# Two projection stages joined: branch and merge gates as one plan of units, each of seven products

## The chip, the cores and the metric

The kernel runs on one core of a Trainium2 chip. The metric is the device time of one execution in microseconds. Shown are the median of three executions and one profiled execution, from which all durations are read.

## The reference, cut to what matters

All of it is in float32, with 2048 latent tokens, width 1024 and two mixers (branches a and b) of 4 heads of 128. The part around the change is the end of the first block:

```
u = layer_norm(x) * (1 + scale) + shift
a_gate, b_gate, merge = columns of (u @ w_in)          # 512, 512 and 2 * 1024 columns
def rms_norm_gated(o, gain, gate):
    return o * rsqrt(mean(o * o) + eps) * gain * silu(gate)
y_a = rms_norm_gated(o_a, a_norm_g, a_gate) @ w_a_out    # o_a, o_b: the mixers' outputs, per head
y_b = rms_norm_gated(o_b, b_norm_g, b_gate) @ w_b_out
gates = sigmoid(merge.reshape(tokens, 2, 1024))
sub = (gates[0] * y_a + gates[1] * y_b) @ w_out
```

Each mixer runs in two directions, and `o_a`, `o_b` are the sums of the two outputs. After this comes a residual, and a second block that the change leaves alone.

## The kernel before, in words

The program is a chain of phases. Each is a block in which every engine has its own hand-written instruction stream, in the order of the code, with waits on counting semaphores; a new block starts on all engines when the old one has ended. PE is TensorE, DVE is VectorE, ACT is ScalarE, POOL is GpSimd, and SP issues most DMAs. A name as `T.at(v, "m4")` is the semaphore value that stands once product m4 of unit v is done. `bank` is PSUM: 8 banks of 128x512 float32.

`uT` holds u, with 8 blocks of 128 rows by 256 context and 2048 latent tokens. Its context columns hold weights by the time of these phases. `phase_scans` loads the first weights there (`wg_saved`) at its end. `yT` receives the normed, turned outputs: 8 heads by 2048 tokens.

**Branch gates** (`phase_branch_gates`). For each of 8 heads f and 4 blocks b of 512 tokens, PE does 8 matmuls (L1614, one for each block of 128 rows of u) and ACT a Silu (L1660). Meanwhile 32 groups of the mixers' outputs are normed. A group goes through these steps: SP loads its two directions (`outputs`, tiles `o` and `other`), DVE adds them (L1668), ACT squares (L1634), DVE reduces, scales and inverts (L1672 to L1677), ACT takes the root (L1637), DVE multiplies (L1681), PE turns it with 4 transposes (L1622) into one of 4 banks, and ACT copies it with the gain into `yT` (L1649). PE turns two groups after each block from the second to the seventeenth. DVE then multiplies `yT` by the Silu (L1689), and SP saves the second half of the tokens to DRAM (`y_d`).

**Merge gates** (`phase_merge_gates`). Here a unit is 256 output columns by 1024 tokens (a half), so 2 by 2 blocks on each side of a product. They are made with seven products of 4 matmuls (Strassen's scheme in Winograd's form, `PRODUCTS`) where eight would be the plain way. POOL makes four sums of the weights (L1769 to L1774) into `S`, which has two buffers; DVE makes four sums of the tokens once for each half (L1833 to L1842), in spare space of `yT`; PE does the products (L1787) and takes a new bank only when that of eight products ago is read; ACT keeps a copy of m1 (L1811); DVE combines the products (L1853 to L1869); ACT applies the Sigmoid (L1820) and stores to `sig_d`. There are 16 units: 8 on the first half of the tokens, 8 on the second.

After it, `phase_merge` uses `yT` and `sig_d`.

## Time and profile before

| | |
|---|---|
| median of 3 executions | 4029.23 us (4026.57 to 4033.26) |
| profiled execution, its own time | 4030.66 us |
| its span | 4028.9 us |
| TensorE busy | 3772.0 us, 94% of the span |
| branch gates | from 1501.7 us on |
| merge gates | from 1747.2 us to 2137.9 us |

The span is that of the instructions in the profile; 1.8 us of the execution's time lie around it. Each float32 matmul stands in the trace as two records (256 matmuls of the branch gates are 512 records), a transpose as one. A matmul's recorded duration overlaps the next one's: the pitch from start to start is what a product costs.

### The profile page before, as it was taken

Reading aid. Unit: us, or ns where it says so; the run is one execution under the profiler, and the core shown is the slowest. Engines: PE = TensorE matmul, PEld = TensorE weight load, DVE = VectorE, ACT = ScalarE, POOL = GpSimd, SP = SyncE. Lnnn points to the kernel's source line nnn. Section 1 sums busy time; section 2 is a strip of 40 time slices with the busy share of each in tenths; the row PEclk is TensorE's granted clock in tenths of the full one; section 3 lists DMA queues with packets and bytes.
Section 4 is the critical chain, followed back from the end, with each engine's and each line's share of the span. In section 5 each row is a group of like instructions: output and inputs, shape, how many; then the busy total and the mean of one; then the engine's idle time right before and its main releaser. Section 6 shows DMA issues by size and latency. Waiting matters only on the chain. (4 is left out here: it accounts for less than half of the span.)

```text
span 4028.9 us, 48826 instructions
## 1 busy us (share of the span) xinstructions
PE 3772.0 (94%) x18971; PEld 1980.1 (49%) x18971; DVE 2214.4 (55%) x3725; ACT 1204.6 (30%) x2355; POOL 727.5 (18%) x660
## 2 busy tenths in 40 slices
PE   6999899999799989999999989899998999999898
PEld 3444354444577764444444434343554355565543
DVE  7688426653466655222225877622456466565578
ACT  3333123454355547301110001111222244444300
POOL 0000000000566650022113332223110000000032
PEclk8999999999899999999999999999998999999999
DMA  5122673567645544222324633321101100000133
GB/s 189 47 50 49 112 150 112 112 123 127 172 158 175 180 140 141 82 73 84 125 84 146 230 105 120 118 96 68 48 32 37 35 1 8 8 1 6 58 125 110
DMA packets 590152, 386.33 MB, mean 96 GB/s; under 512 B 412019, under 2 KB 525783, under 8 KB 586979
## 3 DMA queue, kind: packets, MB, share of 16 engines
q1 hardware_dynamic: 573059, 315.57, 28.4%
q0 software_dynamic: 10336, 42.47, 2.9%
q10 hardware_dynamic: 6528, 25.17, 1.6%
q8 instruction: 152, 2.49, 0.3%
q14 instruction: 77, 0.63, 0.1%
HBM read 252.59 MB, written 130.55 MB: 95 GB/s over the span
## 5 line engine op out<-in xcount | busy, mean ns | idle before, releaser
L632 PE MATMUL bank<-uT,front_W 128*128 128x512 f32 (+1 forms) x1216 | 489.3, 564 | 4.4 <-ACT front_b_ L839 4.4
L564 PE MATMUL bank<-uT,front_W 128*128 128x512 f32 (+1 forms) x896 | 363.5, 564 | 0.0
L632 PEld LDWEIGHTS bank<-uT,front_W 128*128 128x128 f32 x1216 | 232.7, 192 | 252.6 <-issue 246.0
L564 PEld LDWEIGHTS bank<-uT,front_W 128*128 128x128 f32 x896 | 170.0, 191 | 183.1 <-issue 179.8
L3245 PE MATMUL bank<-kT,attn_qT 96*128 96x512 f32 (+3 forms) x640 | 248.6, 540 | 7.6 <-ACT kT L3305 6.8
L1614 PE MATMUL bank<-uT 128*128 128x512 f32 x512 | 224.3, 596 | 4.3 <-PEq L1183 4.3
L3245 PEld LDWEIGHTS bank<-kT,attn_qT 96*128 96x128 f32 x640 | 114.1, 190 | 131.2 <-issue 74.7
L1313 POOL TENSOR_TENSOR scan_U<-scan_U,gla_w 128x512 f32<-128x512 f32 x144 | 146.9, 1041 | 168.8 <-DVE scan_U L1501 168.8
L3365 DVE TENSOR_SCALAR_CACHE_REDUCE attn_sc_big<-bank 128x512 f32<-128x512 f32 (+1 forms) x208 | 125.9, 627 | 72.9 <-PE bank L3245 71.0
L1614 PEld LDWEIGHTS bank<-uT 128*128 128x128 f32 x512 | 96.5, 191 | 119.8 <-issue 119.8
L1303 POOL TENSOR_TENSOR scan_SP<-scan_S,eGl 128x512 f32<-128x512 f32 x144 | 146.9, 1041 | 19.9 <-DVE scan_S L1520 13.6
L3388 DVE COPY attn_pT<-bank 128x512 f32<-128x512 f32 (+1 forms) x184 | 110.3, 635 | 70.8 <-PE bank L3260 70.8
L3314 ACT ACTIVATE attn_sc_big<-attn_sc_big,attn_top 128x1920 f32<-128x1920 f32 (+3 forms) x64 | 104.3, 1629 | 111.2 <-DVE attn_top L3377 111.2
L1009 DVE RECIPROCAL front_q<-front_q 128x2048 f32<-128x2048 f32 (+1 forms) x8 | 110.0, 13752 | 47.5 <-ACT front_q L786 47.5
L3273 PE MATMUL bank<-attn_pT,uT 128*64 128x256 f32 (+1 forms) x1152 | 129.9, 372 | 5.2 <-DVE attn_pT L3388 5.2
L3479 POOL TENSOR_TENSOR out_S<-uT,out_b 128x512 f32<-128x512 f32 x8 | 13.1, 1639 | 671.0 <-DVE uT L3559 671.0
L1520 DVE TENSOR_TENSOR scan_S<-scan_SP,bank 128x512 f32<-128x512 f32 x144 | 92.5, 685 | 63.4 <-PE bank L1395 63.4
L1001 DVE SCALAR_TENSOR_TENSOR front_work<-front_work,front_taps 128x2308 f32<-128x2308 f32 (+1 forms) x48 | 121.6, 2533 | 1.7
L479 POOL TENSOR_TENSOR front_work<-front_neg_beta,ctri 128x256 f32<-128x256 f32 x18 | 13.1, 750 | 594.3 <-DVE front_neg_beta L1065 510.6
L1787 PE MATMUL bank<-yT,merge_S 128*128 128x512 f32 x256 | 116.8, 599 | 2.3 <-POOL merge_S L1774 2.3
L3260 PE MATMUL bank<-ident,attn_sc_big 128*128 128x128 f32 x800 | 103.3, 281 | 15.9 <-DVE attn_pT L3388 12.6
L1820 ACT ACTIVATE merge_r<-merge_r 128x1024 f32<-128x1024 f32 x32 | 33.7, 1052 | 266.6 <-DVE merge_r L1867 264.2
(547 smaller groups left out, 7070.8 us busy)
## 6 DMA issues: line engine op xcount, KB each, us to landing
scan_gq<-gla_asks_keys_values SPq DMA_DIRECT2D x36, 768.0 KB, 7.7
scan_dq<-delta_qkv SPq DMA_DIRECT2D x32, 768.0 KB, 6.2
merge_gates<-merge_r ACTq DMA_DIRECT2D x16, 1024.0 KB
uT<-merge_gates SPq DMA_DIRECT2D x16, 1024.0 KB, 8.8
gla_asks_keys_values<-front_a SPq DMA_DIRECT2D x14, 1152.0 KB, 11.0
front_W<-in_w_in SPq DMA_DIRECT2D x28, 512.0 KB, 10.7
delta_qkv<-front_b_ SPq DMA_DIRECT2D x8, 1152.0 KB, 9.9
gla_asks_keys_values<-front_b_ SPq DMA_DIRECT2D x8, 1152.0 KB, 17.8
```

The costliest lines, as they stand in the source:

```text
L564: m = pe.matmul(bank[:, conv_bank(f, b), 0:n], W[:, f % 2, k, :], uT[:, k, t0:t0 + n], start=(k == 0), stop=(k == KT - 1))
L632: mm = pe.matmul(bank[:, b, 0:n], W[:, s, k, :], uT[:, k, t0:t0 + n], start=(k == 0), stop=(k == KT - 1))
L1001: dve.scalar_tensor_tensor(out=acc[:, lo:WIDE], in0=raw[:, f % 2, lo + t:t + WIDE], scalar=tap[:, t:t + 1], in1=acc[:, lo:WIDE], op0=ALU.m ...
L1009: dve.reciprocal(inv[:, r], inv[:, r]).then_inc(DY("inv"), 1)
L1303: nc.gpsimd.tensor_tensor(SP[d][:], S[d][:], bcast(gl, 2, P), ALU.mult).then_inc(GS(f"SP{d}"), 1)
L1313: nc.gpsimd.tensor_tensor(U[d][:], U[d][:], bcast(w, 2, P), ALU.mult).then_inc(GU(f"U{d}"), 1)
L1614: mm = pe.matmul(bank[:, b, :], W[f % 2][:, k, :], uT[:, k, CTX + b * BANK:CTX + (b + 1) * BANK], start=(k == 0), stop=(k == KT - 1))
L1787: mm = pe.matmul(bank[:, spot(q, name), :], left[:, k, :], right(k), start=(k == 0), stop=(k == H - 1))
L3245: pe.matmul(bank[:, SC0 + ring[name] % NS, 0:hi - lo], qT[:, e, i * P:(i + 1) * P], kT[0:QK, e, lo:hi], start=True, stop=True).then_inc(TS ...
L3273: m = pe.matmul(bank[e * DV:(e + 1) * DV, ob, r0:2 * P], vall[:, c, h * DV:(h + 1) * DV], pT[:, n % NPT, e, r0:2 * P], start=(c == 0), sto ...
L3365: m = dve.tensor_scalar(t[:, g * BANK:g * BANK + w], bk[:, 0:w], SCALE, None, ALU.mult, ALU.max, accum_out=mx[:, s, u, plain:plain + 1])
L3388: dve.tensor_copy(*turned_spot(a, p, c)).then_inc(DT(name), 1)
```

## The change

`phase_branch_gates` and `phase_merge_gates` become one block, `phase_gates`, driven by a list `PLAN` of 24 units of the same shape: 8 merge units of the first half of the tokens, then 8 branch units (a pair of heads by a half), then 8 merge units of the second half. So the branch gates' projections are made in seven products too. The norming and turning of the 32 groups is spread over the first products: step k stands at product 3k/2 (`slot_of`), that is two steps in each three products, with PE's transposes of group k - 3 behind that product. The sum of the two directions moves from DVE to POOL. The transposes have 2 banks and the products 6. `S` has one buffer, and POOL waits for products m5 and m3 of the unit before. The token sums lie in tiles `T1`, `T2`, `T4` of their own and are rebuilt at the three places where the plan turns to the other half (`TURNS`: units 10, 14, 16).

```diff
+    BRANCH = [(0, 0), (1, 0), (1, 1), (0, 1), (2, 1), (3, 1), (3, 0), (2, 0)]
+    merge = lambda g: [("merge", br, j, g) for br in range(2) for j in range(COLS)]
+    PLAN = merge(0) + [("branch", p // (HEADS // 2), p, g) for p, g in BRANCH] + merge(1)
+    UNITS, NBU = len(PLAN), len(BRANCH)
...
+    SLOT = [v % 2 for v in range(NM)] + [0, 1, 1, 0, 1, 0, 0, 1] + [v % 2 for v in range(NM)]
+    SUMS = ["new"] * NM + ["new", "new", "", "again", "new", "new", "", "again"] + ["new"] * NM
+    TURNS = [v for v in range(1, UNITS) if half_of(v) != half_of(v - 1)]
...
+    slot_of = lambda k: 3 * k // 2
+    steps_at = lambda x: [k for k in range(ALL + 3) if slot_of(k) == x]
...
-        W = [uT[:, :, s * P:(s + 1) * P] for s in range(2)]
+        W = [uT[:, :, 0:2 * P], WM]
+        S = sb("S", [P, 3, H, P])
+        T1, T2, T4 = (sb(n, [P, H, BANK]) for n in ("T1", "T2", "T4"))
...
-        sq = sb("sq", [P, 2, GC, P])
...
-        silu = sb("silu", [P, 2, SEQ])
+        r = sb("r", [P, 2, 2, PAIR])
...
+        spot = lambda v, name: (7 * v + PRODUCTS.index(name)) % 6
...
-        @block.gpsimd
-        def _(pool):
-            nc.clear_and_free_semaphores(chip.ended)
...
+                    sp.wait_ge(DI.sem, DI.at(i - 2, "ss"))
...
+            for x in range(7 * UNITS):
+                v, i = divmod(x, 7)
+                for k in steps_at(x):
+                    if 2 <= k + 1 < ALL:
+                        outputs(k + 1)
+                if i == 0:
+                    for n, (w, after) in enumerate(LOADS):
+                        if after is not None and after == v - 1:
+                            weights(n)
...
+            nc.clear_and_free_semaphores(chip.ended)
...
+                    weights_here(pool, v)
+                    if v:
+                        pool.wait_ge(T.sem, T.at(v - 1, "m5"))
+                    pool.tensor_tensor(S[:, 0], w21, w22, ALU.add).then_inc(GW("s1"), 1)
+                    pool.wait_ge(GW.sem, GW.at(n, "s1"))
+                    pool.tensor_tensor(S[:, 1], S[:, 0], w11, ALU.subtract).then_inc(GW("s2"), 1)
+                    pool.tensor_tensor(w21, w11, w21, ALU.subtract).then_inc(GW("s3"), 1)
+                    if v:
+                        pool.wait_ge(T.sem, T.at(v - 1, "m3"))
+                    pool.wait_ge(GW.sem, GW.at(n, "s2"))
+                    pool.tensor_tensor(S[:, 2], w12, S[:, 1], ALU.subtract).then_inc(GW("s4"), 1)
...
+            weights(0)
+            for x in range(7 * UNITS):
+                for i in steps_at(x):
                     if i < ALL:
-                        outputs(i)
-                if B % NB == NB - 1 and B // NB + 2 < NF:
-                    weights(B // NB + 2)
...
-            for f in range(NF):
-                pe.wait_ge(w_loaded[f % 2], f // 2 * 16 + 16)
-                for b in range(NB):
...
-                    for i in turned(f * NB + b):
...
+            def turned(i):
...
+                    tr = pe.transpose(bank[:, 6 + i % 2, c * P:(c + 1) * P], o[:, i % 4, c, :], chip.ident[:])
+                tr.then_inc(TT("turned"), 1)
...
+                x = 7 * v + PRODUCTS.index(name)
+                if x >= 6:
+                    reader, value = taken[PRODUCTS[(x - 6) % 7]]
+                    pe.wait_ge(reader.sem, reader.at((x - 6) // 7, value))
+                for k in range(H):
+                    mm = pe.matmul(bank[:, spot(v, name), :], left[:, k, :], right[:, k, :], start=(k == 0), stop=(k == H - 1))
+                mm.then_inc(T(name), 1)
+                for k in steps_at(x):
+                    if k >= 3:
+                        turned(k - 3)
...
+                weights_here(pe, v)
+                product(v, "m1", w11, u(g, LO, 0))
+                product(v, "m2", w12, u(g, HI, 0))
+                if SUMS[v] == "new":
+                    pe.wait_ge(GW.sem, GW.at(n, "s3"))
+                elif SUMS[v]:
+                    pe.wait_ge(GA.sem, GA.at(n, "s1"))
...
+                if fresh:
+                    pe.wait_ge(DT.sem, DT.at(i, "t2"))
+                product(v, "m6", S[:, 1], T2)
...
+                if SUMS[v] == "new":
+                    pe.wait_ge(GW.sem, GW.at(n, "s4"))
...
+                product(v, "m3", S[:, 2], u(g, HI, 1))
+                if fresh:
+                    pe.wait_ge(DT.sem, DT.at(i, "t4"))
+                product(v, "m4", w22, T4)
...
-                    act.wait_ge(DS.sem, DS.at(i, "sum"))
-                    if i >= 2:
-                        act.wait_ge(DI.sem, DI.at(i - 2, "ss"))
-                    act.activation(sq[:, i % 2], o[:, i % 4], ACT.Square).then_inc(AQ("sq"), 1)
+                    act.wait_ge(GS.sem, GS.at(i, "sum"))
+                    act.activation(other[:, i % 2], o[:, i % 4], ACT.Square).then_inc(AQ("sq"), 1)
...
-            for f in range(NF):
-                for b in range(NB):
-                    B = f * NB + b
-                    for i in (2 * B, 2 * B + 1):
-                        norm(i)
-                    for i in turned(B):
-                        turn(i)
-                    act.wait_ge(T.sem, T.at(f, f"proj{b}"))
-                    if f >= 2:
...
+            for x in range(7 * UNITS):
+                v, i = divmod(x, 7)
+                for k in steps_at(x):
+                    if k >= 3:
+                        turn(k - 3)
+                    norm(k)
+                if i == 0:
+                    keep(v)
+                    if v:
+                        gate(v - 1, 1)
+                if i == 6:
+                    gate(v, 0)
...
-                if i < ALL:
-                    dve.wait_ge(o_loaded[i % 4], i // 4 * 32 + 32)
-                    dve.tensor_tensor(o[:, i % 4], o[:, i % 4], other[:, i % 2], ALU.add).then_inc(DS("sum"), 1)
...
+            def gated(v):
+                _, br, p, g = PLAN[v]
+                dve.wait_ge(AT.sem, AT.at(NG * (1 + br) - 1, "turned"))
+                dve.wait_ge(AS.sem, AS.at(v, "gate1"))
+                y = yT[:, 2 * p:2 * p + 2, g * PAIR:(g + 1) * PAIR]
+                dve.tensor_tensor(y, y, r[:, v % 2], ALU.mult).then_inc(DY("y"), 1)
...
+            for x in range(7 * UNITS):
+                v, i = divmod(x, 7)
+                for k in steps_at(x):
+                    norm(k)
+                if x == 1:
+                    last_sum(0)
+                if x == 3:
+                    difference(1)
+                combine(v, PRODUCTS[i])
+                if i == 2 and v and is_branch(v - 1):
+                    gated(v - 1)
+                if v + 1 in TURNS:
+                    g, n = half_of(v + 1), TURNS.index(v + 1) + 1
+                    if PRODUCTS[i] == "m7":
+                        second_sum(g)
+                    if PRODUCTS[i] == "m3":
+                        first_sum(g, n)
+                    if PRODUCTS[i] == "m4":
+                        last_sum(g)
```

The next rows are TensorE's, at the start of the branch gates (before) and of the joined block (after). L1614 and L1622 are a block's matmuls and the transposes, as above.

```order
L1606 UNCONDITIONAL_BRANCH
L1614 MATMUL bank<-uT 128x512 x16
L1622 MATMUL bank<-ident,gates_o 128x128 x8
L1614 MATMUL bank<-uT 128x512 x8
L1622 MATMUL bank<-ident,gates_o 128x128 x8
L1614 MATMUL bank<-uT 128x512 x8
```

```order
L1710 UNCONDITIONAL_BRANCH
L1726 MATMUL bank<-uT 128x512 x8
L1726 MATMUL bank<-gates_T,gates_S 128x512 x4
L1726 MATMUL bank<-uT 128x512 x4
L1726 MATMUL bank<-gates_T,gates_S 128x512 x4
L1717 MATMUL bank<-ident,gates_o 128x128 x4
L1726 MATMUL bank<-uT,gates_S 128x512 x4
L1726 MATMUL bank<-gates_T,uT 128x512 x4
L1717 MATMUL bank<-ident,gates_o 128x128 x4
L1726 MATMUL bank<-uT,WM 128x512 x4
L1717 MATMUL bank<-ident,gates_o 128x128 x4
L1726 MATMUL bank<-uT,WM 128x512 x4
```

The transposes (now L1717) came in eights behind every block of 8 matmuls; now they come in fours, behind two of each three products of 4 matmuls (L1726). Ahead of the first of them stand five products.

The next rows are GpSimd's, from the same place. The ISA row clears semaphores; before, the second branch is the start of the merge gates, some 250 us later.

```order
L1570 UNCONDITIONAL_BRANCH
L1572 ISA
L1544 UNCONDITIONAL_BRANCH
L1761 UNCONDITIONAL_BRANCH
L1769 TENSOR_TENSOR merge_S<-WM 128x512
L1771 TENSOR_TENSOR merge_S<-merge_S,WM 128x512
L1772 TENSOR_TENSOR WM<-WM 128x4x128
L1774 TENSOR_TENSOR merge_S<-WM,merge_S 128x512
L1769 TENSOR_TENSOR merge_S<-merge_W 128x512
L1771 TENSOR_TENSOR merge_S<-merge_S,merge_W 128x512
L1772 TENSOR_TENSOR merge_W<-merge_W 128x4x128
L1774 TENSOR_TENSOR merge_S<-merge_W,merge_S 128x512
```

```order
L1672 UNCONDITIONAL_BRANCH
L1674 ISA
L1685 TENSOR_TENSOR gates_S<-uT 128x512
L1687 TENSOR_TENSOR gates_S<-gates_S,uT 128x512
L1688 TENSOR_TENSOR uT<-uT 128x4x128
L1692 TENSOR_TENSOR gates_S<-uT,gates_S 128x512
L1706 TENSOR_TENSOR gates_o<-gates_o,gates_other 128x512 x5
L1685 TENSOR_TENSOR gates_S<-WM 128x512
L1687 TENSOR_TENSOR gates_S<-gates_S,WM 128x512
L1688 TENSOR_TENSOR WM<-WM 128x4x128
L1692 TENSOR_TENSOR gates_S<-WM,gates_S 128x512
L1706 TENSOR_TENSOR gates_o<-gates_o,gates_other 128x512 x5
```

The first weight sums (L1685 to L1692) now stand directly behind the clear, and the sums of the mixers' outputs (L1706) stand between the weight sums of one unit and those of the next.

The last rows are ScalarE's: before, in the branch gates; after, around the end of the second merge unit. L1782 copies a turned group, L1767 squares, L1770 is the root, L1788 keeps m1, L1792 is the gate's function and L1797 stores.

```order
L1649 ACTIVATE yT<-bank,gates_gain 128x4x128 x2
L1660 ACT_TABLE_LOAD
L1660 ACTIVATE gates_silu<-bank 128x512
L1634 ACTIVATE gates_sq<-gates_o 128x512
L1637 ACT_TABLE_LOAD
L1637 ACTIVATE gates_ss<-gates_ss 128x4
L1634 ACTIVATE gates_sq<-gates_o 128x512
L1637 ACTIVATE gates_ss<-gates_ss 128x4
```

```order
L1792 ACT_TABLE_LOAD
L1792 ACTIVATE gates_r<-gates_r 128x1024
L1788 ACTIVATE gates_kept<-bank 128x512
L1792 ACTIVATE gates_r<-gates_r 128x1024
L1797 DMA merge_gates<-gates_r 128x2x1024
L1782 ACTIVATE yT<-bank,gates_gain 128x4x128
L1767 ACTIVATE gates_other<-gates_o 128x512
L1770 ACT_TABLE_LOAD
L1770 ACTIVATE gates_ss<-gates_ss 128x4
L1782 ACTIVATE yT<-bank,gates_gain 128x4x128
L1767 ACTIVATE gates_other<-gates_o 128x512
L1770 ACTIVATE gates_ss<-gates_ss 128x4
```

The Silu of a block between steps has gone; the two Sigmoids of a unit and the copy of m1 stand there in its place.

## Rows read from the trace of the kernel before

**Rows 1.** The page: the span, and TensorE (busy us, share, instructions).

```profile
span 4028.9 us, 48826 instructions
PE 3772.0 (94%) x18971; PEld 1980.1 (49%) x18971; DVE 2214.4 (55%) x3725; ACT 1204.6 (30%) x2355; POOL 727.5 (18%) x660
```

**Rows 2.** Timeline of TensorE, branch gates: start, us, what, count.

```profile
1501.72 15.67 PE L1614 MATMUL bank<-uT 128*128 128x512 f32 x32 [4.26 <-PEq L1183]
1517.22 1.04 PE L1622 MATMUL bank<-ident,gates_o 128*128 128x128 f32 x8
1518.10 7.03 PE L1614 MATMUL bank<-uT 128*128 128x512 f32 x16
```

**Rows 3.** Waits, 1480 to 2260 us: total, times, longest, in us.

```profile
PE bank L1622 <- DVE gates_o L1681: 5.4, 8, 1.5
```

**Rows 4.** Timeline of TensorE, merge gates: its first unit and its last product.

```profile
1747.20 8.80 PE L1787 MATMUL bank<-uT,WM 128*128 128x512 f32 x16 [2.15 <-PEq L1544]
1758.31 5.32 PE L1787 MATMUL bank<-yT,merge_S 128*128 128x512 f32 x8 [2.31 <-POOL merge_S L1774]
1763.47 3.60 PE L1787 MATMUL bank<-uT,WM 128*128 128x512 f32 x8
1777.20 5.31 PE L1787 MATMUL bank<-uT,merge_W 128*128 128x512 f32 x12
...
2134.27 3.60 PE L1787 MATMUL bank<-merge_T,merge_W 128*128 128x512 f32 x8
```

**Rows 5.** Windows: length, busy us of PE, PEld, DVE, ACT, POOL; PEclk; DMA.

```profile
1500.00:1505.00 5.00, 3.28 (x5) 1.51 (x6) 0.00 (x0) 0.00 (x0) 0.39 (x1) 0.72 0.42 133
1760.00:1765.00 5.00, 5.00 (x11) 2.19 (x10) 1.70 (x3) 0.00 (x0) 4.92 (x4) 0.84 0.00 0
1501.70:1745.10 243.40, 237.86 (x640) 110.68 (x640) 90.21 (x191) 115.18 (x162) 0.00 (x0) 0.99 0.32 102
```

**Rows 6.** GpSimd and VectorE: timeline rows, and the semaphore clear.

```profile
1751.68 3.31 POOL L1772 TENSOR_TENSOR WM<-WM 128x512 f32<-128x512 f32 x1
1878.67 2.28 DVE L1836 TENSOR_TENSOR uT<-uT 128x2048 f32<-128x2048 f32 x1
1878.88 3.20 POOL L1769 TENSOR_TENSOR merge_S<-WM 128x512 f32<-128x512 f32 x1 [18.85 <-DMA WM<-in_w_in]
1882.16 1.26 POOL L1771 TENSOR_TENSOR merge_S<-merge_S,WM 128x512 f32<-128x512 f32 x1
L1572 POOLq EVENT_SEMAPHORE_RANGE_CLEAR  x1: 439/439/439, 1501.8 to 1501.8; - x1
```

**Rows 7.** ScalarE in the branch gates: groups (busy, mean ns), then timeline.

```profile
L1649 ACT ACTIVATE yT<-bank,gates_gain 128x512 f32<-128x512 f32 x32 | 27.7, 909 | 13.0 <-PE bank L1622 12.8
L1637 ACT ACT_TABLE_LOAD x17 | 21.8, 1283 | 0.3
L1634 ACT ACTIVATE gates_sq<-gates_o 128x512 f32<-128x512 f32 x32 | 20.1, 627 | 22.8 <-DVE gates_o L1668 22.4
1509.59 1.28 ACT L1637 ACT_TABLE_LOAD   x1
1510.89 0.20 ACT L1637 ACTIVATE gates_ss<-gates_ss 128x4 f32<-128x4 f32 x1
```

**Rows 8.** VectorE, groups of 1495 to 2160 us: busy, mean ns, idle before.

```profile
L1672 DVE TENSOR_REDUCE gates_ss<-gates_sq 128x4 f32<-128x512 f32 x32 | 21.7, 679 | 0.4 <-ACT gates_sq L1634 0.4
L1681 DVE TENSOR_TENSOR gates_o<-gates_o,gates_ss 128x512 f32<-128x512 f32 x32 | 21.2, 663 | 5.6 <-ACT gates_ss L1637 5.6
L1677 DVE RECIPROCAL gates_ss<-gates_ss 128x4 f32<-128x4 f32 x32 | 5.7, 178 | 1.1
L1855 DVE TENSOR_TENSOR merge_r<-bank,merge_kept 128x512 f32<-128x512 f32 x16 | 11.1, 692 | 42.0 <-PE bank L1787 42.0
```

**Rows 9.** DMA issues: count, KB each, median us to landing.

```profile
gates_other<-mixer_outputs SPq DMA_DIRECT2D x32, 256.0 KB, 3.2
WM<-in_w_in SPq DMA_DIRECT2D x7, 1024.0 KB, 5.3
```

More of the change, by code:

```diff
@@ L1543, in phase_branch_gates @@
     ALL = 2 * NG
+    COLS = DM // (2 * P)
+    BRANCH = [(0, 0), (1, 0), (1, 1), (0, 1), (2, 1), (3, 1), (3, 0), (2, 0)]
+    merge = lambda g: [("merge", br, j, g) for br in range(2) for j in range(COLS)]
+    PLAN = merge(0) + [("branch", p // (HEADS // 2), p, g) for p, g in BRANCH] + merge(1)
+    UNITS, NBU = len(PLAN), len(BRANCH)
+    NM = 2 * COLS
+    half_of = lambda v: PLAN[v][3]
+    is_branch = lambda v: PLAN[v][0] == "branch"
+    nth = lambda v: [w for w in range(UNITS) if is_branch(w) == is_branch(v)].index(v)
+    SLOT = [v % 2 for v in range(NM)] + [0, 1, 1, 0, 1, 0, 0, 1] + [v % 2 for v in range(NM)]
+    SUMS = ["new"] * NM + ["new", "new", "", "again", "new", "new", "", "again"] + ["new"] * NM
+    TURNS = [v for v in range(1, UNITS) if half_of(v) != half_of(v - 1)]
+    LOADS = [(v, max([w for w in range(v) if SLOT[w] == SLOT[v]], default=None)) for v in range(1, UNITS) if SUMS[v] == "new"]
+    LOADS.sort(key=lambda load: -1 if load[1] is None else load[1])
+    arrivals = {}
+    for n, (v, after) in enumerate(LOADS):
+        arrivals[v] = 16 * (2 + sum(SLOT[w] == SLOT[v] for w, a in LOADS[:n]))
+    slot_of = lambda k: 3 * k // 2
+    steps_at = lambda x: [k for k in range(ALL + 3) if slot_of(k) == x]
     with ExitStack() as st:
@@ L1574, in _, with weights @@
         @block.sync
         def _(sp):
-            def weights(f):
-                if f >= 2:
-                    sp.wait_ge(T.sem, T.at(f - 2, f"proj{NB - 1}"))
-                base = C_AGATE if f < HEADS else C_BGATE - HD
-                sp.dma_start(W[f % 2], w_in[:, base + f * P:base + (f + 1) * P].rearrange("(k p) n -> p k n", p=P)
-                             ).then_inc(w_loaded[f % 2], 16)
+            def weights(n):
+                v, after = LOADS[n]
+                if after is not None:
+                    sp.wait_ge(T.sem, T.at(after, "m4"))
+                kind, br, p, g = PLAN[v]
+                if kind == "branch":
+                    c = (C_AGATE if br == 0 else C_BGATE - HD) + 2 * p * P
+                else:
+                    c = C_MERGE + br * DM + p * 2 * P
+                sp.dma_start(W[SLOT[v]], w_in[:, c:c + 2 * P].rearrange("(k p) n -> p k n", p=P)
+                             ).then_inc(w_loaded[SLOT[v]], 16)
@@ new lines, in _, with weights @@
+            sp.wait_ge(T.sem, T.at(UNITS - 2, "m4"))
+            for br, w in enumerate((w_a_out, w_b_out)):
+                sp.dma_start(uT[:, br * HEADS:(br + 1) * HEADS, 0:2 * P], w[:, 0:2 * P].rearrange("(k p) n -> p k n", p=P)
+                             ).then_inc(wy_loaded, 16)
+            sp.wait_ge(wy_loaded, 32)
+            sp.wait_ge(y_loaded, 16 * 2 * HEADS)
+        @block.gpsimd
+        def _(pool):
+            nc.clear_and_free_semaphores(chip.ended)
+            def weights(v):
+                if not SUMS[v]:
+                    return
+                w11, w12, w21, w22 = quarters(v)
+                n = SUMS[:v].count(SUMS[v])
+                if SUMS[v] == "new":
[10 more added lines that the diff above has]
+                    pool.tensor_tensor(S[:, 2], w12, S[:, 1], ALU.subtract).then_inc(GW("s4"), 1)
+                else:
+                    pool.wait_ge(T.sem, T.at(v - 1, "m5"))
+                    pool.tensor_tensor(S[:, 1], w22, w21, ALU.subtract).then_inc(GA("s2"), 1)
+                    pool.wait_ge(GA.sem, GA.at(n, "s2"))
+                    pool.tensor_tensor(S[:, 0], S[:, 1], w11, ALU.add).then_inc(GA("s1"), 1)
+                    pool.wait_ge(T.sem, T.at(v - 1, "m3"))
+                    pool.tensor_tensor(S[:, 2], w12, S[:, 1], ALU.subtract).then_inc(GA("s4"), 1)
+            weights(0)
+            for x in range(7 * UNITS):
+                for i in steps_at(x):
+                    if i < ALL:
+                        pool.wait_ge(o_loaded[i % 4], i // 4 * 32 + 32)
+                        pool.tensor_tensor(o[:, i % 4], o[:, i % 4], other[:, i % 2], ALU.add).then_inc(GS("sum"), 1)
+                if x % 7 == 6 and x // 7 + 1 < UNITS:
+                    weights(x // 7 + 1)
@@ new lines, in product @@
+            def product(v, name, left, right):
+                x = 7 * v + PRODUCTS.index(name)
[8 more added lines that the diff above has]
+                        turned(k - 3)
@@ L1671, in norm @@
                     dve.wait_ge(AQ.sem, AQ.at(n, "sq"))
[L1672 removed]
+                    dve.tensor_reduce(ss[:, n, 0, :], other[:, n % 2], AX.X, ALU.add).then_inc(DI("ss"), 1)
                     dve.wait_ge(DI.sem, DI.at(n, "ss"))
```

335 lines of the change are left out of this document (120 added, 215 removed).

## The prediction

> **What bounds the kernel now.** I read the page first: TensorE is busy 3772.0 of 4028.9 us, no other engine above 55% [rows 1]. Then the timeline of TensorE over the two stages: it runs from 1501.72 us to the end of the last product, 2134.27 + 3.43 = 2137.70 us, with hardly a gap [rows 2, 4]. In the branch gates it is busy 237.86 of 243.40 us [rows 5]. So this stretch of 636.0 us costs what TensorE's instructions cost, plus a few named waits, and a change here is worth what it does to TensorE's instructions and to those waits. The other engines matter only where they are late.
>
> **The pitch of a product.** From the start of m1 of the second merge unit (1777.20) to the start of the last m4 (2134.27) are 357.07 us and 104 products [rows 4]: 3.433 us a product, 0.858 us a matmul, 24.03 us a unit. The branch gates' matmuls have the same size (128x128 by 512), and I give them the same price.
>
> **Where the 636.0 us go before.** Branch gates, 243.4 us: 256 matmuls x 0.858 = 219.7. The first 16 of them took 1517.22 - 1501.72 = 15.50 where 13.73 is the price, 1.8 too much; the granted clock of that time is 0.72 of full in the first window, so TensorE was for a part of it at 1.2 GHz, after it had stood still for 4.26 us [rows 2, 5]. Transposes: 8 in 1518.10 - 1517.22 = 0.88 us, 0.44 a group, 14.1 for 32 groups [rows 2]. What is left, 7.8 us, is waiting: 5.4 us are booked as waits of the transposes for VectorE's scaled group [rows 3]; the other 2.4 I take for refilling behind them. Merge gates: 2.15 us at the block's boundary. The first unit took 1777.20 - 1747.20 = 30.00 us, 5.97 over its price: m1 and m2 8.80 for 6.87, a wait of 2.31 for GpSimd's weight sums, and m6 5.16 for 3.43 [rows 4], the granted clock being still at 0.84 behind that wait [rows 5]. Then 15 units x 24.03 = 360.5. Sum: 243.4 + 2.15 + 30.0 + 360.5 = 636.05, as the timeline has it.
>
> **What the change removes on TensorE.** The same projections in 24 units of 28 matmuls are 672 for 256 + 448 = 704: 32 matmuls, 27.5 us. The 32 groups of transposes stay, 14.1 us. They now stand alone in fours where they came in eights; if all of the 2.4 us above is really the price of breaking the stream, they cost 16.5. I take 14.1, since in the rows with no wait the eight cost only 0.88.
>
> **The start, which stays once.** One of two starts goes, with its 2.15 us boundary. The remaining one looks like the merge gates' start. m1 and m2 cost 15.50 - 6.87 = 8.6 us (to 1510.35) for 6.87, so 1.8 over. GpSimd clears semaphores until 1502.2 [rows 6], then makes three sums before m6 may start. VectorE makes three token sums of 2.28 us at the same time. The rows show what such a meeting does: a GpSimd sum that takes 1.26 us alone took 3.20 when it began 0.2 us behind a VectorE sum of 2.28, and 3.31 in the merge gates' start [rows 6]. In turns, GpSimd ends at about 1505.3, 1508.8 and 1512.3. So m6 waits 2.0 us, and then has m6's 1.7 us of low clock again. Start cost: 1.8 + 2.0 + 1.7 = 5.5 us. Bounds: 1.8 if GpSimd is in time, 8.1 if it costs what the merge gates' start did with its boundary.
>
> **What is laid beside TensorE, and whether it stays there.** During the steps a unit costs TensorE 24.03 + 4.67 groups x 0.44 = 26.1 us. *VectorE*: a step is 0.68 + two small ones of about 0.18 + 0.66 = 1.7 us, and a unit has 4.67 of them and seven combining operations of 0.69 [rows 8]: 12.8 us. *ScalarE*: 4.67 x (0.91 + 0.63 + 0.20) = 8.1, the copy of m1 and two Sigmoids about 2.7 together (0.6 and twice 1.05, by size), and three table loads of 1.28 [rows 7], 3.9: 14.7 us. *GpSimd*: four weight sums of 1.27 and 4.67 output sums of at most the same: 11 us. None is a bound by its load; what counts is order. I cost at nothing, with its cover: the weights' loads (5.3 us to landing [rows 9], one unit of 24 us to land in); the weight sums with one buffer (allowed from the end of m5, wanted by m6 four products or 13.7 us later, 3.8 us of work); the token sums at the three turns (2.28 us each, wanted five products later); the products' six banks (a reader has five products, 17 us, where it had seven); the branch units' multiplications and saves; the loads for the next stage, issued one unit before the end. Without its cover each would stop TensorE for its own length.
>
> **The tight places.** (1) Group 0 is turned behind the fifth product. By my count its sum comes behind the four weight sums (1514.7), its square at 1515.3, VectorE then makes a token sum and two combinations, and the scaled group is there at 1523. TensorE is there at 1512.4 + 5.2 + 6.9 = 1524.5: 1.5 us of slack. (2) In units 1 and 4 the output sum of the seventh product's step stands on GpSimd ahead of the next unit's weight sums. Counted from the end of m5: a load may start at 3.9 (behind m3 and a turned group) and lands near 7.8 (two issues, then 3.2 us [rows 9]), the output sum ends at 9, three weight sums at 12.8 to 13; m6 wants them at 15.1. Two us of slack. (3) SP issues a unit's weights behind a step's loads, which wait for the turned group: at most 4 us late, of some 18 spare. For (1) to (3) together I set 1.0 us of waiting.
>
> Whether a scaling multiply of 0.66 us (a tile and a broadcast column, both in SBUF) also blocks GpSimd is in no row. The Trainium skill, "SBUF — State Buffer", its part on engine ports, says that any VectorE instruction with two SBUF inputs and a GpSimd instruction that reads SBUF exclude each other for the whole instruction; by it each multiply that meets a sum adds up to 0.66 us, 3.1 us over a unit, and place (2) would lose most of its slack. A second rule speaks against ScalarE: "ScalarE: Activation LUTs", What ACT_TABLE_LOAD costs, gives 2.66 us for a switch of tables, a drain of 1.38 included. Here the load begun at 1509.59 lasts 1.28, and the root starts at 1510.89, right behind it [rows 7]: this trace does not show that drain. With it ScalarE's unit would be 18.8 us, still below 26.1, but its burst at a unit's edge would be longer than the distance to the next step.
>
> **Sum.** After: 576.7 + 14.1 + 5.5 + 1.0 = 597.3. Before: 636.05. Gain 38.7 us: 27.5 from matmuls, 6.8 from the transposes' waits, 4.4 from the starts (1.8 + 2.15 + 5.97 - 5.5). From the profiled execution's 4030.66 us that gives 3992.0. That execution stands 1.4 us above the median of the three, so by the median 3990.5. I say 3991.
>
> **The rivals.**
> *A, the forecast*: TensorE stays the bound. With the bounds above (start 1.8 to 8.1, transposes 14.1 to 16.5, waits 0 to 3) the gain is 32 to 43 us: 3986 to 3997. Chance 0.75.
> *B, the cover is thin*: a GpSimd sum or a scaled group is late in several of the seven mixed units, and each wait also lowers the clock. Priced by the merge gates' start, 2.31 + 1.73 = 4.0 us a time; at three places 12 us, 4003; at all seven 28 us, 4019. For it: slacks of 1.5 to 2 us, against an estimate with as much error. Against it: no load above 60% of the unit, and every queue can catch up. Chance 0.2, most of it near 4000.
> *C, slower*: the steps' loop itself is too long. `o` has four buffers, so group i + 4 is loaded only when group i is turned, and four steps are six products, 20.6 + 1.8 = 22.4 us. Bare, the loop is 0.8 issue + 3.2 landing + 1.3 + 0.6 + 1.1 + 1.5 + 0.7 = 9.2 us. Each engine holds other work ahead of it (GpSimd up to 5 us of weight sums, ScalarE 4, VectorE 3). If queueing made it 30 us, TensorE would wait 7.6 us each four steps, 61 us in 32 steps: 4052. It turns slower than before from a loop of 27.3 us on (39 us of waiting). Chance 0.03.
> *D, nothing gained beyond the matmuls*: the starts and waits stay what they were and only 27.5 us go: 4002, inside B's span. *E*: the first unit hardly waits, and the gain is 43 us or more: 0.02.
>
> **Range and chances.** 3986 to 4001 leaves out C, the upper part of B and a little of A. A measurement of this kernel tells 0.2%, 8 us, from no change. Faster by more: A, E and nearly all of B, 0.96; within: 0.02; slower: C's larger part, 0.02.
>
> **What would show it right or wrong.** The product pitch in all 24 units at 3.43 us; TensorE's stretch from m1 of unit 0 to the last m4 near 597 us and 672 matmuls; m6 of unit 0 waiting about 2 us for a GpSimd sum, with the granted clock near 0.8 around it; waits of the transposes for the scaled group near nothing; a unit in the mixed part at 26.1 us. Wrong would be: units 1 to 6 longer than 27 us, with waits on `gates_S` or `gates_o` (B), or the wait of every step's loads on SP handed through to TensorE (C); a pitch above 3.43; or a next stage that begins with a longer gap.

## The result and the profile after

The changed kernel took 3985.55 us (median of 4 runs, 3984.27 to 3988.39), the kernel before, on the same chip, 4029.55 us (4 runs, 4026.57 to 4033.26). The ratio is 0.9891, 95% interval 0.9874 to 0.9908: 44.0 us less. The prediction was 3991, its range 3986 to 4001: the time lies just below the range. The profiled execution took 3984.89 us, its span is 3983.1.

The page of the changed kernel, the lines that answer to [rows 1]:

```profile
span 3983.1 us, 48748 instructions
PE 3738.3 (94%) x18907; PEld 1965.4 (49%) x18907; DVE 2257.9 (57%) x3731; ACT 1188.4 (30%) x2336; POOL 789.7 (20%) x714
```

There are 64 TensorE records fewer, two for each of the 32 matmuls that are gone, and 54 more on GpSimd, mostly the 32 output sums. TensorE's busy time fell by 33.7 us, the span by 45.8: the rest of the gain is standing time.

The timeline of TensorE in the changed kernel: the start of the joint stage, its last product, and the first instructions of the next two stages.

```profile
1501.79 8.77 PE L1726 MATMUL bank<-uT 128*128 128x512 f32 x16 [4.50 <-PEq L1183]
1511.56 3.70 PE L1726 MATMUL bank<-gates_T,gates_S 128*128 128x512 f32 x8 [1.00 <-POOL uT L1688]
1515.09 3.60 PE L1726 MATMUL bank<-uT 128*128 128x512 f32 x8
1518.53 3.60 PE L1726 MATMUL bank<-gates_T,gates_S 128*128 128x512 f32 x8
1521.96 0.60 PE L1717 MATMUL bank<-ident,gates_o 128*128 128x128 f32 x4
1522.40 3.60 PE L1726 MATMUL bank<-uT,gates_S 128*128 128x512 f32 x8
...
2092.21 3.60 PE L1726 MATMUL bank<-gates_T,WM 128*128 128x512 f32 x8
2102.16 4.23 PE L2028 MATMUL bank<-yT,uT 128*128 128x512 f32 x5 [6.36 <-PEq L1568]
2311.45 2.04 PE L2251 MATMUL bank<-yT 128*128 128x512 f32 x2 [10.75 <-PEq L1914]
```

Read the starts: 1515.09, 1518.53, 1521.96 are 3.43 us apart, the pitch of a product as before [rows 4], and the four transposes between 1521.96 and 1522.40 cost 0.44. The stretch from the first m1 to the end of the last m4 is 2092.21 + 3.43 - 1501.79 = 593.85 us, where [rows 2, 4] give 635.98.

The same next stages in the kernel before, from the timeline of TensorE:

```profile
2144.26 4.33 PE L1995 MATMUL bank<-yT,uT 128*128 128x512 f32 x6 [6.40 <-PEq L1713]
2355.81 2.05 PE L2218 MATMUL bank<-yT 128*128 128x512 f32 x2 [10.74 <-PEq L1881]
```

From these rows the span's 45.8 us divide by place. From the first m1 to the next stage's first matmul: 642.54 against 600.37 us, 42.2 gained. That next stage to the following one: 211.55 against 209.29, 2.3 gained. Everything behind it: 4028.9 - 2355.81 = 1673.09 against 3983.1 - 2311.45 = 1671.65, 1.4 gained. The change's own stretch holds 42.2; the other 3.7 are in stages whose work it doesn't touch (0.1 us was lost ahead of the stretch).

The waits of the changed kernel, 1495 to 2110 us (total, times, longest):

```profile
PEld bank L1717 <- DVE gates_o L1830: 0.2, 1, 0.2
POOL gates_o L1706 <- DMA gates_other<-mixer_outputs: 85.6, 23, 8.6
ACT gates_other L1767 <- POOL gates_o L1706: 33.0, 11, 17.5
```

Where [rows 3] had 5.4 us of transposes waiting for the scaled group, 0.2 is left. GpSimd stands 85.6 us for the mixers' outputs, up to 8.6 at a time. ScalarE, which squares a group next, waits for these sums in turn (33.0 us), but the groups are still ready when TensorE comes, so none of this waiting reaches TensorE. Who waits for a load turned out to be the point of the experiments below.

### The profile page after: what moved, and what is told of

The parts are those of the page before. It is cut to its first block and busy times, and to the rows that moved or that the text cites. A ratio compares the mean times of both kernels' runs of the same rounds, so it can differ in the third digit from the quotient of the medians.

```text
span 3983.1 us, 48748 instructions
## 1 busy us (share of the span) xinstructions
PE 3738.3 (94%) x18907; PEld 1965.4 (49%) x18907; DVE 2257.9 (57%) x3731; ACT 1188.4 (30%) x2336; POOL 789.7 (20%) x714
## 3 DMA queue, kind: packets, MB, share of 16 engines
q8 instruction: 151, 2.47, 0.3%
## 5 line engine op out<-in xcount | busy, mean ns | idle before, releaser
L1726 PE MATMUL bank<-gates_T,gates_S 128*128 128x512 f32 x384 | 172.7, 592 | 1.0 <-POOL uT L1688 1.0
L1726 PE MATMUL bank<-uT 128*128 128x512 f32 x288 | 129.6, 599 | 4.5 <-PEq L1183 4.5
L1792 ACT ACTIVATE gates_r<-gates_r 128x1024 f32<-128x1024 f32 x48 | 50.6, 1054 | 270.0 <-DVE gates_r L1879 267.5
L1726 PE MATMUL bank<-uT,WM 128*128 128x512 f32 x288 | 128.0, 592 | 0.0
```

Source lines behind the costliest of these rows:

```text
L1726: mm = pe.matmul(bank[:, spot(v, name), :], left[:, k, :], right[:, k, :], start=(k == 0), stop=(k == H - 1))
```

## The experiments

In all of them "the stretch" is the time from the first m1 (in the kernel before, the first matmul of the branch gates) to the end of the last m4, by the timeline of TensorE. One execution of the changed kernel has 593.85 us of it, the other 593.94 (below), so differences of 0.5 us in it can be read, where the medians of whole runs scatter by several us.

**Both kernels once more.** No edit. The kernel before, one run:

> The kernel before, unchanged, for a second profile. The change gained 42.1 us between the first product of the gates and the last, and 3.7 us more behind it (2.2 of them in the stage that follows, 200.2 against 197.9 us from its first to its last product). Theory (chance): the stages behind the gates differ from one execution to the next by 1 to 3 us, in waits for DMA, so this profile shows the stage behind the gates anywhere from 197.5 to 200.5 us. Rival (the change speeds up what follows): again 200.2 within 0.4 us.

It took 4029.3 us. Its stretch begins with the same record and ends 2132.92 + 3.43 = 2136.35, 635.3 us long. The start of its merge gates, in the timeline of TensorE, differs from [rows 4]:

```profile
1745.77 7.10 PE L1787 MATMUL bank<-uT,WM 128*128 128x512 f32 x16 [2.15 <-PEq L1544]
1756.88 5.40 PE L1787 MATMUL bank<-yT,merge_S 128*128 128x512 f32 x8 [4.01 <-POOL merge_S L1774]
1762.12 3.60 PE L1787 MATMUL bank<-uT,WM 128*128 128x512 f32 x8
2142.92 4.65 PE L1995 MATMUL bank<-yT,uT 128*128 128x512 f32 x6 [6.40 <-PEq L1713]
2354.36 2.05 PE L2218 MATMUL bank<-yT 128*128 128x512 f32 x2 [10.73 <-PEq L1881]
```

The same boundary of 2.15 us did not slow m1 and m2 here (7.10 us; in [rows 4] 8.80). They ended 1.7 us earlier, and m6 then waited 1.7 us longer (4.01 for 2.31) for the same GpSimd sum: from m1 to m6 are 11.11 us in both. So the low clock of m1 and m2 was no cost of its own: the sums set the start. What cost was the sum's lateness and m6's own low clock.

The changed kernel, four runs:

> The changed kernel, unchanged, for a second profile and a narrower interval. Both theories: 3985.5 us within 1.5, the gates' stretch 593.9 us within 0.5. Theory (chance): the stage behind the gates takes anywhere from 197.5 to 200.5 us. Rival (the change speeds up what follows): 197.9 again within 0.4, and the time behind the last product of the gates is 3.5 us shorter than in both profiles of before.

3985.36 us (3983.43 to 3989.32) against 4026.3 (4024.04 to 4028.14), ratio 0.9897 [0.988, 0.9913]; here the gain is 40.9 us. Rows of the timeline of TensorE:

```profile
1502.26 8.74 PE L1726 MATMUL bank<-uT 128*128 128x512 f32 x16 [4.42 <-PEq L1183]
1512.12 3.70 PE L1726 MATMUL bank<-gates_T,gates_S 128*128 128x512 f32 x8 [1.12 <-POOL uT L1688]
2092.77 3.60 PE L1726 MATMUL bank<-gates_T,WM 128*128 128x512 f32 x8
2102.72 4.59 PE L2028 MATMUL bank<-yT,uT 128*128 128x512 f32 x6 [6.35 <-PEq L1568]
2314.39 2.05 PE L2251 MATMUL bank<-yT 128*128 128x512 f32 x2 [10.76 <-PEq L1914]
```

The gates' start repeats, and the next stage does not: 2314.39 - 2102.72 = 211.67 us in this execution of the same kernel, 209.29 in the first, 211.55 and 211.44 in the two of the kernel before. The kernel before with its output sums on GpSimd (below) has 209.07 us there. What came out 2.3 us better behind the gates in the first pair is scatter from execution to execution, not the change; the last section shows where in that stage it arises. Between this pair the gain up to the next stage's start is 641.88 - 600.46 = 41.4.

**Is it the matmuls?** The 32 matmuls are put back: each of the eight branch units makes its m1 (4 matmuls) twice.

```
-                for k in range(H):
-                    mm = pe.matmul(bank[:, spot(v, name), :], left[:, k, :], ...)
+                for again in range(2 if name == "m1" and is_branch(v) else 1):
+                    for k in range(H):
+                        mm = pe.matmul(bank[:, spot(v, name), :], left[:, k, :], ...)
```

> In the eight branch units product m1 is made twice, the second time over the first, so the joined stage has the 704 matmuls that the two stages had. Theory (the 32 matmuls are worth their pitch of 0.858 us and nothing else): 27.5 us slower than the changed kernel, 4013, and still 14.5 us faster than before; the gates' stretch 621.4 us. Rival (the eight-product form was not priced at the seven-product pitch, or part of the 27.5 hides in waits): under 25 or over 30 us.

4013.72 us (4013.1 to 4017.0, 6 runs) against 4026.46 (15 runs), ratio 0.9967 [0.9955, 0.998]. The stretch runs from 1503.45 to 2121.43 + 3.43, 621.41 us: 27.5 more than without. So 27.5 us of the gain are the matmuls; the 12.7 us that this kernel is still faster (by the stretch 14.6, against the first profile of the kernel before) are the rest, waits and starts.

**The wait of m6 in the first unit.** In the changed kernel m6 waits for the third of the sums that GpSimd makes. Here it waits for the fourth in unit 0.

```
-                    pe.wait_ge(GW.sem, GW.at(n, "s3"))
+                    pe.wait_ge(GW.sem, GW.at(n, "s3" if v else "s4"))
```

> In unit 0 alone TensorE waits for the fourth weight sum before m6, not for the third, as the merge gates did before. The fourth ends 1.2 us later, so the wait before m6 grows from 1.0 to 2.2 us. Theory (a longer wait brings the low clock with it, as in the kernel before: 2.31 us of waiting, then 1.7 us lost in m6): 2.9 us slower, 3988.5, m6 of unit 0 at 5.2 us and not 3.5. Rival (the low clock came from what TensorE did before the block began, not from this wait): 1.2 us slower, 3986.8, m6 at 3.5 us.

3987.16 us (3985.95 to 3988.7), ratio 0.9903 [0.9888, 0.9918]. TensorE's timeline:

```profile
1512.61 3.70 PE L1726 MATMUL bank<-gates_T,gates_S 128*128 128x512 f32 x8 [2.19 <-POOL gates_S L1692]
1516.14 3.60 PE L1726 MATMUL bank<-uT 128*128 128x512 f32 x8
```

A standstill of 2.19 us, and m6 behind it takes 1516.14 - 1512.61 = 3.53, the full rate. The stretch grew by 1.2 us, the wait alone. The prediction's step "a wait of two us brings 1.7 us of low clock" does not hold here.

**Longer waits at the same place.** Two kernels in which m6 of unit 0 also waits for GpSimd's first output sum (the first expectation) or second (the second):

```
+                if v == 0:
+                    pe.wait_ge(GS.sem, GS.at(0, "sum"))      # second kernel: GS.at(1, "sum")
```

> In unit 0, m6 waits besides for GpSimd's first sum of the mixers' outputs, so TensorE stands still for some 3.4 us and not 1.0 after its first 16 records. Waits of 1.0 and 2.2 us there left the clock at full and m6 at 3.53 us; a wait of 4.0 us in the second profile of before cost m6 5.24 us. Theory (the clock falls by the length of the standstill, and the bound lies between 2.2 and 4.0): m6 either 3.5 or 5.2 us, the gates' stretch 2.4 or 4.1 us longer than 593.5. Rival (at this place the clock does not fall, since what counts is something else than the wait): m6 3.5 here and in the next kernel too.

> The same with GpSimd's second sum: a standstill of some 4.6 us. Theory (a standstill of 4 us or more brings the low clock): m6 about 5.2 us and not 3.5, the gates' stretch 3.6 + 1.7 = 5.3 us longer than 593.5. Rival: m6 3.5 us, the stretch 3.6 us longer.

One run each: 3984.93 and 3991.81 us. The timeline of TensorE in the first:

```profile
1511.08 3.67 PE L1726 MATMUL bank<-gates_T,gates_S 128*128 128x512 f32 x8 [3.01 <-issue]
1514.59 3.60 PE L1726 MATMUL bank<-uT 128*128 128x512 f32 x8
```

In the second:

```profile
1513.94 5.37 PE L1726 MATMUL bank<-gates_T,gates_S 128*128 128x512 f32 x8 [4.77 <-issue]
1519.15 3.60 PE L1726 MATMUL bank<-uT 128*128 128x512 f32 x8
```

And the window of the second at the start of m6 (columns as in [rows 5]):

```profile
1514.00:1516.00 2.00, 2.00 (x3) 0.88 (x4) 1.93 (x4) 1.97 (x3) 0.00 (x0) 0.56 0.42 114
```

A standstill of 3.01 us left the clock full (m6 3.51); one of 4.77 us ended with m6 at 5.21 and a granted clock of 0.56 in this window, near the lower of the two levels (1.2 GHz of 2.4). The stretch grew by 2.4 and 5.4 us. In the first that is 2.0 of added wait and 0.5 of m1 and m2, which took 9.24 us in this execution; in the second 3.8 of wait and 1.7 of clock.

**Removing the wait of m6.** VectorE makes its third token sum only behind GpSimd's third weight sum:

```
             second_sum(0)
+            dve.wait_ge(GW.sem, GW.at(0, "s3"))
             first_sum(0, 0)
```

> VectorE makes its third token sum only when GpSimd has made its third weight sum, in unit 0 alone. Theory (the two engines exclude each other, so the third weight sum then takes 1.27 us and not 3.3): it is ready at about 1509.5, m6 starts with no wait at 1510.6, 1.0 us faster: 3984.5; the groups behind are not late. Rival (the sum is slow for another reason, or the token sum comes too late for m5 and moves the wait there): no gain, 3985.5 or slower.

3985.46 us (3983.79 to 3986.67), ratio 0.9898 [0.9883, 0.9913]. GpSimd's timeline in the changed kernel:

```profile
1502.28 2.69 POOL L1685 TENSOR_TENSOR gates_S<-uT 128x512 f32<-128x512 f32 x1 [2.06 <-POOLq L1183]
1505.04 3.19 POOL L1687 TENSOR_TENSOR gates_S<-gates_S,uT 128x512 f32<-128x512 f32 x1
1508.20 3.31 POOL L1688 TENSOR_TENSOR uT<-uT 128x512 f32<-128x512 f32 x1
```

And with the edit, the third sum and TensorE:

```profile
1499.95 8.80 PE L1726 MATMUL bank<-uT 128*128 128x512 f32 x16 [4.41 <-PEq L1183]
1506.45 1.26 POOL L1688 TENSOR_TENSOR uT<-uT 128x512 f32<-128x512 f32 x1
1508.59 3.60 PE L1726 MATMUL bank<-gates_T,gates_S 128*128 128x512 f32 x8
```

The third sum took 1.26 us where it took 3.31, and m6 started behind m2 without a wait. The stretch is 592.98 us, the shortest of all, 0.9 less. The medians of whole runs (3985.46 and 3985.36) cannot tell 1 us, so this is the better version by its trace alone.

**What the move of the output sums to GpSimd is worth, twice.** First in the kernel before: its direction sums go to GpSimd, which was idle there.

```
+            for i in range(ALL):
+                pool.wait_ge(o_loaded[i % 4], i // 4 * 32 + 32)
+                pool.tensor_tensor(o[:, i % 4], o[:, i % 4], other[:, i % 2], ALU.add).then_inc(DS("sum"), 1)
...
             def norm(i):
-                if i < ALL:
-                    dve.wait_ge(o_loaded[i % 4], i // 4 * 32 + 32)
-                    dve.tensor_tensor(o[:, i % 4], o[:, i % 4], other[:, i % 2], ALU.add).then_inc(DS("sum"), 1)
```

> The kernel before with one part of the change alone: the sum of the two directions of the mixers' outputs on GpSimd, idle in that stage, and not on VectorE. Theory (the transposes' waits of before came from the pairs of groups behind one block of 6.9 us, that is from the spacing of the steps): the waits shrink by at most half, 1 to 4 us faster than before. Rival (they came from VectorE's load): all 7.8 us go, 7 us or more faster.

4023.39 us (4019.91 to 4027.77, 10 runs) against 4026.46, ratio 0.9994 [0.9985, 1.0004]: no difference that can be told. The transposes wait less (the waits, 1480 to 2260 us, that answer to [rows 3]):

```profile
PE bank L1625 <- DVE gates_o L1681: 3.8, 4, 1.4
```

From the first matmul to the boundary it needs 241.4 us, the two executions of the kernel before 243.3 and 242.6: 1.2 to 1.9 us less. That is the theory's size, not the rival's 7 us or more.

Then in the changed kernel: the sums go back to VectorE, ahead of the step's other work (removed from GpSimd's loop).

```
             def norm(i):
+                if i < ALL:
+                    dve.wait_ge(o_loaded[i % 4], i // 4 * 32 + 32)
+                    dve.tensor_tensor(o[:, i % 4], o[:, i % 4], other[:, i % 2], ALU.add).then_inc(GS("sum"), 1)
                 n = i - 1
```

> The changed kernel with the sums of the mixers' outputs back on VectorE. Theory (moving them bought nothing, VectorE's load is 13 of 26 us and the spacing does the work): the gates' stretch within 1.5 us of 593.9. Rival (the move to GpSimd is what removed the waits): VectorE waits for each load in its place in line, TensorE's transposes wait again, 5 us or more slower.

3992.01 us (2 runs), ratio 0.9912 [0.9892, 0.9932], and a stretch of 601.93 us, 8.0 longer. My expectation fell. The waits of this kernel:

```profile
PE bank L1713 <- DVE gates_o L1829: 6.0, 7, 2.0
PEld bank L1713 <- DVE gates_o L1829: 13.5, 9, 2.8
DVE gates_o L1816 <- DMA gates_other<-mixer_outputs: 62.3, 22, 6.6
```

VectorE now stands 62.3 us for the loads. One such place in its timeline, and TensorE behind it:

```profile
1573.98 0.69 DVE L1816 TENSOR_TENSOR gates_o<-gates_o,gates_other 128x512 f32<-128x512 f32 x1 [6.46 <-DMA gates_other<-mixer_outputs]
1575.60 0.66 DVE L1829 TENSOR_TENSOR gates_o<-gates_o,gates_ss 128x512 f32<-128x512 f32 x1
1576.32 0.66 PE L1713 MATMUL bank<-ident,gates_o 128*128 128x128 f32 x4 [0.26 <-DVE gates_o L1829]
```

VectorE stood 6.46 us for a load of a later group. The multiply that scales an earlier group was queued behind it, came at 1575.60, and TensorE took the group 0.06 us after its end. If this is the cause, the sum's place in the step matters and its engine does not. The next kernel has the same block on VectorE at the end of the step:

```
                     dve.tensor_tensor(o[:, n % 4], o[:, n % 4], bcast(ss[:, n, 3, :], 2, P), ALU.mult).then_inc(DO("o"), 1)
+                if i < ALL:
+                    dve.wait_ge(o_loaded[i % 4], i // 4 * 32 + 32)
+                    dve.tensor_tensor(o[:, i % 4], o[:, i % 4], other[:, i % 2], ALU.add).then_inc(GS("sum"), 1)
```

> The sums of the mixers' outputs on VectorE, but in each step behind the scaling multiply and not ahead of the reduction. Theory (with the sum first, VectorE's wait for a load, up to 6.5 us behind a weights' load, holds up the multiply of a group that is ready, and TensorE's transposes with it): those waits go, the gates' stretch is 593 to 596 us where the sum in front gave 601.5. Rival (VectorE has too much to do, or is locked out by GpSimd, wherever the sum stands): 600 or more.

3984.28 us (2 runs), ratio 0.9898 [0.987, 0.9927]; the stretch is 2088.86 + 3.43 - 1498.35 = 593.94, the 8.0 us are back, and VectorE's wait for loads is

```profile
DVE gates_o L1829 <- DMA gates_other<-mixer_outputs: 8.6, 8, 1.9
```

So the cause of the 8.0 us is shown: the in-order wait for a load ahead of a ready group's steps on VectorE. The load on VectorE, some 22 us more over the stretch, costs nothing.

**How much the spacing of the steps gives.** A step at every product instead of two at every three:

```
-    slot_of = lambda k: 3 * k // 2
+    slot_of = lambda k: k
```

> The steps of the norming stand behind every product, not behind two of three, so four steps have 15.5 us where they had 22.4. Theory (the loop of a group, load to transpose, is some 10 to 13 us with its queueing, so it does not bound TensorE): the gates' stretch stays within 3 us of 593.9, with a few waits of the transposes at the units' edges, where ScalarE has two gates and up to four table loads. Rival (the slack of the change was thin): 10 us or more slower.

3999.2 us (2 runs), ratio 0.993 [0.991, 0.995]; the stretch is 608.72 us, 14.9 longer, where I had said within 3. The waits:

```profile
PEld bank L1717 <- DVE gates_o L1830: 19.5, 12, 3.2
PE bank L1717 <- DVE gates_o L1830: 11.4, 6, 2.4
```

(The two rows overlap: a weight load that waits holds up the matmul behind it.) So here the loop of a step does hold up TensorE. To ask what makes it so, the same kernel with `Copy` for `Sigmoid` in the first eight units. It leaves out the Sigmoid of the first half's merge gates, and with it nearly all the table loads between steps (3 are left in the stretch where the dense kernel has 20):

```
-                act.activation(r[:, v % 2, n, :], r[:, v % 2, n, :], ACT.Silu if is_branch(v) else ACT.Sigmoid
+                act.activation(r[:, v % 2, n, :], r[:, v % 2, n, :], ACT.Copy if v < NM else ACT.Silu if is_branch(v) else ACT.Sigmoid
```

> The dense steps (one behind every product) with Copy in place of the Sigmoid in the first eight units, so ScalarE loads no table there but the root's; this leaves the first half's merge gates without their Sigmoid. Theory (the 14.8 us that the dense steps cost are ScalarE's burst at the units' edges, 12 us of work in two products with its table loads): most of it goes, the gates' stretch within 4 us of 593.5. Rival (the loop from load to transpose is longer than 15.5 us for another reason, the loads behind weights and stores): 604 or more.

3994.3 us (2 runs), ratio 0.9923, a stretch of 604.01 us:

```profile
PE bank L1717 <- DVE gates_o L1830: 7.2, 5, 2.8
```

ScalarE's table loads account for 4.7 of the 14.9 us. The other 10.2 stay, and neither theory has the number right. The loads of the outputs' second direction land 3.1 us after their issue in the median of both kernels, at most 4.6 in the dense one and 7.9 in the one with `Copy`, but no run separated SP's order, the landing and the chain itself; what makes up the 10.2 us is open.

## Where the prediction was right, and which terms were off

*The bound.* Right. TensorE's instructions set the stretch: 593.85 us are 672 x 0.858 = 576.7, transposes 14.1, 3.0 of start and nearly nothing else.

*The matmuls, 27.5 us.* Right, and shown by putting them back: 27.5.

*The transposes, 14.1 us.* Right: 0.44 us also when four stand alone. The upper bound of 16.5 was not needed: the terms just added up leave no room for it, so the 2.4 us that were left over in the branch gates went with the waits.

*The transposes' waits, 6.8 us of gain with 1.0 us left over for the three tight places.* 7.6 instead: only 0.2 us of waiting is in the trace. The new spacing of the steps does not do it alone: with the output sums back at VectorE's place ahead of the multiply, 8.0 us return, as much waiting as before. The move does not do it alone either: in the kernel before it took 1.2 to 1.9 us away. Only together do they bring 7.6. I had put the price of that move at nothing either way and had seen GpSimd's idle time as mere cover. The prediction's C counted the loop's length, and missed which engine waits for the load with what behind it.

*The start, 5.5 us: the term that was mis-sized, and the main one.* It measured 3.0: m1 and m2 1.8 over as predicted, m6's wait 1.1 (1.00 in the profile's own count) for 2.0, m6's low clock 0.1 for 1.7. The wait was shorter because each of GpSimd's three sums took less than the turn I had given it (2.69, 3.19 and 3.31 us for 3.1, 3.5 and 3.5), so that they ended at 1511.51 where I had 1512.3. The low clock was an error of reading: from one row of 2.31 us of waiting with 5.16 us behind it [rows 4] I made a rule for a wait of two us. Waits of 1.0, 2.2 and 3.0 us at this place brought no low clock and 4.8 us did, as did 4.0 us at the merge gates' start in the kernel before, second profile. With that term at 3.0 instead of 5.5 and the waits at 0.2 instead of 1.0, the sum gives 42 us of gain, what the stretch shows.

*The rest.* 42 us off the 4029.23 that I started from is 3987, inside the range. The median fell another 2 us below that. So of the 5.3 us by which the gain passed the forecast's 38.7, the start is 2.5, the waits are 0.8, and 2.0 lie outside the stretch. Stages behind the gates came out 3.7 us shorter in the first pair of profiles; the second pair has none of it (1673.14 and 1673.11 us behind the second stage's start, 211.44 and 211.67 before it) and a gain of 40.9 us by medians. That scatter belongs in a range, and mine had been built from bounds of terms alone. It should have had 2 or 3 us more on either side.

*The rivals.* A, the forecast, holds in mechanism, with its terms near their lower ends. B, thin cover, did not happen: the places had slack, though not much (a step at every product costs 14.9 us). C, the loop as the bound, shows in the dense kernel and not in this one. D is refuted by the kernel with the 32 matmuls put back, which is still 12.7 us faster than before. E, the first unit hardly waits, came nearer than its 0.02: one us of waiting, and a gain of 44.0 by the first medians and 40.9 by the second.

*The ports.* The prediction left open whether a scaling multiply also blocks GpSimd. It does, and GpSimd blocks it too: the instruction that starts second is the one that waits. VectorE's timeline in the changed kernel:

```profile
1524.69 0.66 DVE L1830 TENSOR_TENSOR gates_o<-gates_o,gates_ss 128x512 f32<-128x512 f32 x1
1527.98 1.16 DVE L1823 TENSOR_SCALAR gates_ss<-gates_ss 128x4 f32<-128x4 f32 x1
1529.27 1.62 DVE L1830 TENSOR_TENSOR gates_o<-gates_o,gates_ss 128x512 f32<-128x512 f32 x1
1533.40 1.62 DVE L1830 TENSOR_TENSOR gates_o<-gates_o,gates_ss 128x512 f32<-128x512 f32 x1
```

And GpSimd's:

```profile
1527.85 1.26 POOL L1706 TENSOR_TENSOR gates_o<-gates_o,gates_other 128x512 f32<-128x512 f32 x1 [3.31 <-DMA gates_other<-mixer_outputs]
1529.07 1.26 POOL L1685 TENSOR_TENSOR gates_S<-WM 128x512 f32<-128x512 f32 x1
1534.42 1.73 POOL L1706 TENSOR_TENSOR gates_o<-gates_o,gates_other 128x512 f32<-128x512 f32 x1
```

The same multiply takes 0.66 us alone and 1.62 when it starts 0.2 us behind a GpSimd sum: it ends at 1530.89, 0.56 us behind that sum's end at 1530.33. The other way round, GpSimd's output sum starts at 1534.42, while the multiply begun at 1533.40 runs until 1535.02, and it takes 1.73 us for 1.26. The rule in the Trainium skill, "SBUF — State Buffer", on engine ports (two SBUF inputs on VectorE against a GpSimd instruction that reads SBUF) is borne out by these rows. It did not change the time, since the group was still ready before TensorE came.

## What to carry to other kernels

When transfers land late and irregularly, put the wait for a load on an engine's queue behind everything that is already ready, or on an engine with nothing urgent behind it: here the same sum on the same engine cost 8.0 us or nothing by its place in the step alone. When an engine's instruction stream is the bound, count the instructions that a fusion removes and price them by their pitch; that term was exact, while the start, the waits and the scatter of other stages carried the error. Before a wait is priced with a slow clock behind it, look at more than one such wait, and give a range the scatter of the untouched stages too.

## What the hardware showed beyond the expectation

- TensorE after a standstill at the start of m6: behind 1.00, 2.19 and 3.01 us a product took 3.5 us (2.4 GHz), behind 4.01 and 4.77 us 5.2 us (granted clock 0.67 over the product, so 1.2 GHz for a part of it). But in the first profile of the kernel before 2.31 us were enough for 5.16 [rows 4], with a gap of 2.15 and a low clock 8.8 us earlier. The length of the wait alone is not the rule, and what is, stays open.
- The same gap of 2.15 us at a block's boundary slowed the two products behind it in one profile of the kernel before (8.80 us), and neither in its other profile (7.10) nor in the kernel before with its sums on GpSimd (7.11). The gaps of 4.26 to 4.50 us at the first block's start slowed the first products every time: in the eleven profiles of the changed kernel and its variants m1 and m2 have 8.74 to 8.80 us in the record eight times, and 9.24, 9.95 and 10.09 in the other three, where the price of both is 6.87. With 9.95 (`Copy`) and 10.09 (32 matmuls put back) m6 did not wait at all, so that m1, m2 and m6 together took 13.3 and 13.4 us, as in the two executions of the changed kernel.
- A VectorE instruction on 128x4 elements went from 0.17 us (at 1524.39) to 1.16 beside a GpSimd sum (L1823 above): it ended at 1529.14, the sum at 1529.11. So a small instruction can pay for what is left of the other's turn.
- A stage with the same instructions took 209.3 and 211.7 us in two executions of the same kernel, with TensorE busy 195.26 and 196.97 us over the same 448 records. The difference is at one place. In the first execution:

```profile
2267.85 1.95 PE L2028 MATMUL bank<-yT,branch_S 128*128 128x512 f32 x4 [1.77 <-DVE branch_ra L2095]
```

And in the second:

```profile
2269.08 2.71 PE L2028 MATMUL bank<-yT,branch_S 128*128 128x512 f32 x4 [2.47 <-DVE branch_ra L2095]
```

TensorE waits 0.7 us longer for VectorE there, and the eight records from this start took 5.20 us where they took 3.51: 1.7 us of low clock. All fourteen profiles divide at this wait. Behind standstills of 2.10, 2.12, 2.14, 2.24 and 2.47 us the eight records took 5.2 us and the stage 211.4 to 211.7; in the other nine, behind 1.53 to 1.96 us and once 2.27, they took 3.5 and the stage 209.1 to 210.5. Both kinds of stage occur with the kernel before's code and with the changed one's. The 2.27 us of the kernel with the 32 matmuls put back is again the case that keeps the length alone from being the rule.
